# Differential attention and a convolution norm in a two-block transformer kernel: a group's end in three parts, the norm's small sums in two units

## What is computed

```python
def conv_mixer(u, w, b, gn_g, gn_b):          # 256 channels, 4 groups, 31 taps
    a, gt = jnp.split(u, 2, axis=-1)
    z = a * jax.nn.sigmoid(gt)
    y = causal_depthwise_conv(z, w) + b
    yf = y.reshape(B, S, CONV_GROUPS, CONV_CH // CONV_GROUPS)
    mu = jnp.mean(yf, axis=-1, keepdims=True)
    var = jnp.mean(jnp.square(yf - mu), axis=-1, keepdims=True)
    yn = ((yf - mu) * lax.rsqrt(var + EPS)).reshape(B, S, CONV_CH) * gn_g + gn_b
    return jax.nn.silu(yn)

def diff_attention(q, k, v, ...):             # 4 heads, two maps (m) each, D = 64
    s = jnp.einsum('bhmqd,bhmkd->bhmqk', qb, kh) * scale    # per block of 128 queries
    s = jnp.where(k_pos[None, :] <= q_pos[:, None], s, -jnp.inf)
    p = jax.nn.softmax(s, axis=-1)
    a = p[:, :, 0] - lam * p[:, :, 1]
    o = jnp.einsum('bhqk,bhkv->bhqv', a, vh)
    o = rms_norm_2(o, subln_g) * (1.0 - lambda_init)
```

## Time and profile before

| | us |
|---|---|
| median of three runs | 2995.51 |
| lowest and highest run | 2993.77, 3003.24 |
| span of the profiled execution | 3009.3 |
| PE busy in the span | 2916.2 |
| DVE, ACT, POOL busy | 1520.2, 1212.6, 1162.8 |

### The profile page before, as it was taken

The page is one execution under the profiler, slowest core; times in us unless marked ns, Lnnn a source line. Parts: engine busy times, 40 slices in busy tenths (PEclk is TensorE's granted clock), DMA queues, the critical chain, the costliest instruction groups (busy, mean ns, idle before and its releaser), DMA issues.

```text
span 3009.3 us, 37747 instructions
## 1 busy us (share of the span) xinstructions
PE 2916.2 (97%) x13529; PEld 2341.0 (78%) x13529; DVE 1520.2 (51%) x2650; ACT 1212.6 (40%) x1851; POOL 1162.8 (39%) x598
## 2 busy tenths in 40 slices
PE   9999999999999999999999999999999999997997
PEld 7888888767888888888888867778888777775664
DVE  4441365556744414344145655764441888457665
ACT  4332233665343322433232476443331353425563
POOL 4444353522454443544444351354454332012221
PEclk9999999999999999999999999999999999699998
DMA  4333232202323332333323311423332121016995
GB/s 151 97 98 107 82 130 82 63 25 89 114 91 98 103 106 64 98 98 98 104 83 123 91 41 36 126 81 105 98 104 96 52 88 57 22 63 247 344 359 196
DMA packets 118574, 324.15 MB, mean 108 GB/s; under 512 B 12464, under 2 KB 48688, under 8 KB 117936
## 3 DMA queue, kind: packets, MB, share of 16 engines
q1 hardware_dynamic: 109024, 305.17, 31.2%
q10 hardware_dynamic: 2800, 8.91, 0.8%
q0 software_dynamic: 6624, 8.41, 0.8%
HBM read 313.52 MB, written 24.64 MB: 112 GB/s over the span
## 4 chain that ended last, share of the span: by engine, by line
PE 85%; DVE 7%; ACT 3%; issue 2%; DMA 1%; POOL 1%; DVEq 0%; SPq 0%; ACTq 0%; POOLq 0%
PE ps L430 19%; PE ps L431 19%; PE ps L433 19%; PE ps L465 4%; PE ps L2165 3%; PE ps L1042 2%; PE ps L930 2%; PE ps L2151 1%; PE ps L2153 1%; PE ps L2152 1%; PE ps L1026 1%; PE ps L573 1%; PE ps L492 1%; PE ps L2137 1%; PE ps L919 1%
## 5 line engine op out<-in xcount | busy, mean ns | idle before, releaser
L2913 POOL TENSOR_TENSOR wlo<-raw,whi 128x1024 fp32r<-128x1024 f32 (+1 forms) x368 | 953.7, 2593 | 1415.5 <-ACT whi L628 1415.3
L628 ACT ACTIVATE whi<-raw 128x1024 fp32r<-128x1024 f32 (+1 forms) x368 | 409.2, 1112 | 693.1 <-PE ps L433 585.8
L430 PE MATMUL ps<-xlo,whi 128*128 128x512 f32 x1704 | 665.2, 390 | 2.2 <-POOL wlo L2913 1.6
L431 PE MATMUL ps<-xhi,wlo 128*128 128x512 f32 x1704 | 663.2, 389 | 0.0
L433 PE MATMUL ps<-xhi,whi 128*128 128x512 f32 x1704 | 420.8, 389 | 0.0
L430 PEld LDWEIGHTS ps<-xlo,whi 128*128 128x128 f32 x1704 | 320.0, 188 | 70.0 <-POOL wlo L2913 2.0
L433 PEld LDWEIGHTS ps<-xhi,whi 128*128 128x128 f32 x1704 | 319.8, 188 | 66.3
L431 PEld LDWEIGHTS ps<-xhi,wlo 128*128 128x128 f32 x1704 | 319.9, 188 | 65.9
L430 PE MATMUL ps<-hlo,whi 128*128 128x512 f32 x704 | 277.3, 394 | 0.0
L431 PE MATMUL ps<-hhi,wlo 128*128 128x512 f32 x704 | 275.5, 391 | 0.0
L760 DVE SCALAR_TENSOR_TENSOR xa<-ps,xa 128x512 f32<-128x512 f32 x48 | 33.1, 689 | 353.4 <-PE ps L433 350.6
(11 more groups left out here) (631 smaller groups left out, 4880.8 us busy)
## 6 DMA issues: line engine op xcount, KB each, us to landing
raw<-in_gu SPq DMA_DIRECT2D x176, 512.0 KB, 3.5
raw<-in_mix SPq DMA_DIRECT2D x96, 512.0 KB, 3.6
mraw<-in_w SPq DMA_DIRECT2D x23, 2048.0 KB, 12.4
raw<-in_dn SPq DMA_DIRECT2D x64, 704.0 KB, 4.1
mdraw<-in_w SPq DMA_DIRECT2D x23, 1024.0 KB, 13.5
raw<-in_w SPq DMA_DIRECT2D x32, 512.0 KB, 3.5
gate_rows<-tails SPq DMA_DIRECT2D x32, 256.0 KB, 4.3
sgmn<-gate_rows SPq DMA_DIRECT2D x16, 512.0 KB, 4.0
```

Source lines behind the costliest of these rows:

```text
L430: nc.tensor.matmul(out, whi[:, slot, cols], rlo, start=first and t == 0, stop=False)
L431: nc.tensor.matmul(out, wlo[:, slot, cols], rhi, start=False, stop=False)
L628: nc.scalar.activation(whi[:, s, 0:n], raw[:, r, 0:n], ACT.Copy).then_inc(hi_done, 1)
L2913: nc.gpsimd.tensor_tensor(wlo[:, s, 0:n], raw[:, r, 0:n], whi[:, s, 0:n].bitcast(F32), ALU.subtract).then_inc(w_ready, 1)
```

## The change

A group's end is done in three parts: the first (reciprocals and the first weighted half) behind the maximum at which all of it stood before, the second (the other half and the addition) behind the next maximum, the third (the two sums of squares) behind the one after. The convolution norm's mean moves from u = 4 to u = 5 (`CONV_MEAN`), its sixteen small sums at u = 8 become eight at u = 9 and eight at u = 10, in different banks, and the roots, two in place of one, are taken by ACT at u = 10, which PE's units 11 and 12 wait for. DVE's reciprocal and both copies stand at u = 11 (before: u = 9 and 10). ACT's casts in the units move from u = 1, 4, 8, 12, 16 to u = 4, 6, 9, 13, 16.

```diff
 def dve_units(..., steps=1):
-        for u in range(n + lag):
+        for u in range(n + lag + steps - 1):
...
-            t = u - lag
-            if t >= 0 and t % per == per - 1:
-                dve.wait_ge(S["o_ready"], t + 1)
-                grp = t // per
-                finish(grp, stat[:, 32 + 16 * (grp % 2):32 + 16 * (grp % 2) + per])
+            for step in range(steps):
+                t = u - lag - step
+                if 0 <= t < n and t % per == per - 1:
+                    grp = t // per
+                    sums = stat[:, 32 + 16 * (grp % 2):32 + 16 * (grp % 2) + per]
+                    if step == 0:
+                        dve.wait_ge(S["o_ready"], t + 1)
+                    if steps == 1:
+                        finish(grp, sums)
+                    else:
+                        finish(grp, sums, step)
...
+    OUT_CAST = (6, 9, 13, 16)
...
-        if u == CONV_MEAN + 3:
+        if u == CONV_MEAN + 2:
             pe.wait_ge(S["norm_dve"], 1)
...
-    CONV_MEAN, CONV_AT = 4, 12
+    CONV_MEAN, CONV_AT = 5, 12
...
-        if u == CONV_MEAN + 4:
-            pe.wait_ge(S["sq_ready"], 2)
-            for k in range(2):
-                for kt in range(QT):
-                    at_ = 256 + 8 * k + 2 * kt
-                    ins = nc.tensor.matmul(ps[2][:, at_:at_ + 2], rs2[:, k, kt * P:(kt + 1) * P],
-                                           c("blk64")[:, 0:128:64], start=True, stop=True)
+        k = u - CONV_MEAN - 4
+        if k in (0, 1):
+            pe.wait_ge(S["sq_ready"], k + 1)
+            for kt in range(QT):
+                at_ = 256 + 2 * kt
+                ins = nc.tensor.matmul(ps[2 + u % 2][:, at_:at_ + 2], rs2[:, k, kt * P:(kt + 1) * P],
+                                       c("blk64")[:, 0:128:64], start=True, stop=True)
             ins.then_inc(S["stat_used"], 1)
-        if u == CONV_MEAN + 6:
-            pe.wait_ge(S["std_ready"], 1)
+        if k in (2, 3):
+            pe.wait_ge(S["std_ready"], k - 1)
...
-        if u == 1:
+        if u == 4:
             hi(act, B2, N_IN2_TILES + 3, 0, 8)
...
-        if u == CONV_MEAN + 4:
-            act.wait_ge(S["stat_used"], 1)
-            nc.scalar.activation(conv_r, ps[2][:, 256:272], ACT.Sqrt, bias=eps_ap(RMS_EPS)).then_inc(S["std_ready"], 1)
+        if u == CONV_MEAN + 5:
+            for k in range(2):
+                act.wait_ge(S["stat_used"], k + 1)
+                nc.scalar.activation(conv_r[:, 8 * k:8 * k + 8], ps[2 + (u + 1 + k) % 2][:, 256:264], ACT.Sqrt,
+                                     bias=eps_ap(RMS_EPS)).then_inc(S["std_ready"], 1)
...
-        if u % 4 == 0 and 4 <= u <= 16:
-            hi(act, B2, G2_OUT + u // 4 - 1, 0, 8)
+        if u in OUT_CAST:
+            hi(act, B2, G2_OUT + OUT_CAST.index(u), 0, 8)
...
-        if u == CONV_MEAN + 5:
-            dve.wait_ge(S["std_ready"], 1)
+        if u == CONV_MEAN + 6:
+            dve.wait_ge(S["std_ready"], 2)
             own.link(nc.vector.reciprocal(conv_r, conv_r))
             own.wait()
...
+        def finish_dif(grp, sums, step):
...
+            if step == 0:
+                own.link(nc.vector.reciprocal(w, sums))
+                own.wait()
+                own.link(nc.vector.tensor_tensor(w2[:, :, 1], w2[:, :, 1], small[:, 4:5].broadcast_to([P, 2]), ALU.mult))
+                own.wait()
+                own.link(weighted(0))
+            elif step == 1:
+                weighted(1).then_inc(S["o_used"], 1)
+                dve.wait_ge(S["o_used"], grp + 1)
+                own.wait()
+                own.link(nc.vector.tensor_tensor(o, o, other, ALU.add))
+            else:
+                own.wait()
+                for h in range(2):
+                    r = 4 * (grp // 2) + 2 * (grp % 2) + h
+                    own.link(nc.vector.tensor_tensor_reduce(sg[:, 0, 256 + P * h:256 + P * h + P], o[:, h, :], o[:, h, :],
+                                                           1.0, 0.0, ALU.mult, ALU.add, rt3[:, r:r + 1]))
```

More of the change, by code:

```diff
@@ L953, in act_units, with dve_units @@
                 between(u)
-    def dve_units(dve, units, scale, per, finish, own, s_ring=s_ring, between=None):
+    def dve_units(dve, units, scale, per, finish, own, s_ring=s_ring, between=None, steps=1):
         n = len(units)
         lag = 4
-        for u in range(n + lag):
+        for u in range(n + lag + steps - 1):
             if u < n:
@@ L2036, in dve_late @@
             cols = slice(256 * half, 256 * half + 256)
-            nc.vector.tensor_tensor(cacc[:, 1, cols], cacc[:, 1, cols], ps[2 + half][:, 256:512], ALU.subtract
+            nc.vector.tensor_tensor(cacc[:, 1, cols], cacc[:, 1, cols], ps[2 + u % 2][:, 256:512], ALU.subtract
                                     ).then_inc(S["norm_dve"], 1)
-        if u == CONV_MEAN + 5:
-            dve.wait_ge(S["std_ready"], 1)
+        if u == CONV_MEAN + 6:
+            dve.wait_ge(S["std_ready"], 2)
             own.link(nc.vector.reciprocal(conv_r, conv_r))
             own.wait()
-        if u in (CONV_MEAN + 5, CONV_MEAN + 6):
-            k = u - CONV_MEAN - 5
-            nc.vector.tensor_copy(rs2[:, k, :].rearrange("p (a c) -> p a c", c=64),
-                                  conv_r[:, 8 * k:8 * k + 8].unsqueeze(2).broadcast_to([P, 8, 64])
-                                  ).then_inc(S["conv_wide"], 1)
+            for k in range(2):
+                nc.vector.tensor_copy(rs2[:, k, :].rearrange("p (a c) -> p a c", c=64),
+                                      conv_r[:, 8 * k:8 * k + 8].unsqueeze(2).broadcast_to([P, 8, 64])
+                                      ).then_inc(S["conv_wide"], 1)
         if CONV_AT <= u < CONV_AT + 4:
@@ L2521, in between @@
             dve_late(dve, own, u)
-        def finish_dif(grp, sums):
+        def finish_dif(grp, sums, step):
             w = stat[:, 104:108]
-            own.link(nc.vector.reciprocal(w, sums))
-            own.wait()
             w2 = w.rearrange("p (h m) -> p h m", m=2)
-            own.link(nc.vector.tensor_tensor(w2[:, :, 1], w2[:, :, 1], small[:, 4:5].broadcast_to([P, 2]), ALU.mult))
-            own.wait()
             o = o_dif[:, grp // 2, 256 * (grp % 2):256 * (grp % 2) + 256].rearrange("p (h d) -> p h d", d=P)
@@ L2531, in finish_dif @@
             other = sg[:, 0, 0:256].rearrange("p (h d) -> p h d", d=P)
-            for m in range(2):
-                ins = nc.vector.tensor_tensor((o, other)[m], dif_bank(grp, 0)[:, 256 * m:256 * m + 256].rearrange("p (h d) -> p h d", d=P),
-                                              w2[:, :, m:m + 1].broadcast_to([P, 2, P]), ALU.mult)
-                if m == 0:
-                    own.link(ins)
-                else:
-                    ins.then_inc(S["o_used"], 1)
-            dve.wait_ge(S["o_used"], grp + 1)
@@ L2540, in finish_dif, with weighted @@
-            own.wait()
-            own.link(nc.vector.tensor_tensor(o, o, other, ALU.add))
-            own.wait()
-            for h in range(2):
-                r = 4 * (grp // 2) + 2 * (grp % 2) + h
-                own.link(nc.vector.tensor_tensor_reduce(sg[:, 0, 256 + P * h:256 + P * h + P], o[:, h, :], o[:, h, :], 1.0,
-                                                       0.0, ALU.mult, ALU.add, rt3[:, r:r + 1]))
-        dve_units(dve, dif_units, dif_scale, 4, finish_dif, own, s2_ring, between=between)
+            def weighted(m):
+                return nc.vector.tensor_tensor((o, other)[m],
+                                               dif_bank(grp, 0)[:, 256 * m:256 * m + 256].rearrange("p (h d) -> p h d", d=P),
+                                               w2[:, :, m:m + 1].broadcast_to([P, 2, P]), ALU.mult)
@@ L2548, in dve_second @@
+        dve_units(dve, dif_units, dif_scale, 4, finish_dif, own, s2_ring, between=between, steps=3)
         own.wait()
```

2 lines of the change are left out of this document (1 added, 1 removed).

## The result

The kernel with the change takes 2984.35 us (median of 8 runs, 2979.55 to 2989.09). The kernel before, run beside it, takes 2999.89 (8 runs, 2993.72 to 3013.20; the three runs known ahead are among them). The ratio is 0.9946, with a 95% interval of 0.9927 to 0.9965: some 16 us faster. The four later batches of this study hold 98 runs of the kernel before, with a median of 3000.8 (2988.8 to 3011.1); the change has a median of 2985.0 over all its 16 runs, 15.9 less. The forecast was 2981.8 us, and it named "faster" as likeliest.

A forecast was written before the change was run, and what follows sets the result against it. TensorE was taken as the bound, busy 2916.2 of 3009.3 us. Terms -7.7 - 1.7 + 1.3 - 1.1 - 4.5 = -13.7 us, carried over to the median 2995.5, gave 2981.8 us; 8 in 10 range 2965 to 2996.

The forecast's parts named there:

- Taps and mean: -7.7: Convolution taps of u = 1 and the mean's products: taps 2.1 us shorter, TensorE's clock stays up; -7.7 us.
- "-3" for the case without the clock: At the taps, if the clock falls all the same: only 2.1 us of taps and about 1 of reordering, -3.
- Sums and roots: -1.7 + 1.3 = -0.4: Small sums from u = 8: no clock fall behind them, -1.7 us; new TensorE wait for the root at u = 11, +1.3.
- Group's end: -1.1: Units 15 to 17: split end cuts TensorE's wait for unit 14's copy from 1.50 to about 0.4 us; -1.1 us.
- the early-fall rival: Attention tail: POOL's low part delays the sums of squares at u = 17, clock falls; 2986.3 us; 0.27 with fall at taps.
- the port: DVE instructions with two SBUF inputs and SBUF-reading GpSimd share a port; a rule against the change at the casts' units.
- To the states: -4.5: From 2585.2 us to the state products: no clock fall, -5.7, less a longer wait for values' rows, +1.2; -4.5 us.
- Behind that: 0: Behind the state products: clock falls at ACT's tables and sigmoids, then all goes as before to 2639.8; 0 us.
- the rival of a clock that stays up: Clock stays up to the attention stage's end: another -14 us, 2967.7 us; chance 0.13.
- The carrying over: Whole kernel: the sum from the profiled span, -13.7 us, applied unchanged to the runs' median 2995.5, giving 2981.8 us.
- The slower case: Root wait at u = 11 brings the clock down, work between 2572 and 2585 doubles, +12.7 + 1.3; 3007.4 us; chance 0.06.

The follow-up runs named there:

- second look at before: The kernel before, unchanged, run again for a second profile; 2993.52 us.
- the end whole: The changed kernel with the group's end in one piece again behind one maximum, casts and norm as in the change; 2993.42 us, ratio 0.9981.
- full-clock execution: The changed kernel, unchanged, run again for a second profile, its whole attention stage at full clock; 2985.41 us, ratio 0.9940.

## Why the prediction held, step by step

**Taps and mean: -7.7, and 8.0 in the profile.** The mark at u = 8 moves by 9.8 us (32.7 to 22.9), of which 1.84 are the small sums that now stand behind it. The tap time (2.73) and the first wait (1.15 forecast, 1.17 measured) came as said, and the mean's products waited for nothing. The second look at before shows what it is made of: 3.7 us are clock and the other 4.3 the shorter taps and the order. Where I put "-3" for the case without the clock, it is -4.3. In medians, undoing the casts costs 7.9 and undoing the norm 4.2.

**Sums and roots: -1.7 + 1.3 = -0.4, and -0.3 in the profile.** From u = 8 to 12 it takes 13.6 us in place of 12.1, with 1.9 us of small sums more in it. The root wait was 1.46 for 1.3. But the reason for the -1.7 fails: in the second look at before the clock did not fall there and the four units took 12.0 us, as long as with the fall. ACT's copy at u = 10 set the pace, and a wait of 1.16 took the place of the low time. The low stretch had cost nothing. What paid for the root's wait was something I had not counted: the cast of u = 8 had stood in ACT between the root and the exponential's table, and with the casts moved alone the four units take 11.0 us and the wait of 1.16 is gone. That the sum came out is chance.

**Group's end: -1.1, and -1.34.** 0.16 us of wait for my 0.4. The sums of squares took 0.28 us each, ended 0.2 us before POOL's low part at u = 17 and held nobody up, so the early-fall rival did not come. They did not run side by side, so this place shows nothing of the port. The Trainium skill (SBUF — State Buffer, "Who interferes with whom") says that whichever of the two starts first has the port; the profile with the end whole agrees: there POOL's low part starts 0.64 us ahead of the addition, keeps its usual 2.39 us, and the addition, 2.03 us in place of 0.42, ends 0.3 us behind it. In runs the split is worth more than this term: 8.4 us of the median. What is more than the wait goes with the falls that it keeps away, which the sum carries in the next term.

**To the states: -4.5.** I expected no fall at 2585.2 (right) and a wait of 1.7 for the values' rows (1.45 measured). To the maximum of u = 20 the terms make -8.1 - 1.1 - 4.4 (half of the 8.85 us from 2585.2 to 2594.05) = -13.6; the mark moved by 13.2.

**Behind that: 0, and -11.6 in the profile.** Here the step fails. The clock fell where I said, behind ACT's tables, but "from then to 2639.8 all goes as before" did not hold: it rose after 6.8 us in one execution and did not fall in the other. The profile is therefore nearer to the rival of a clock that stays up. That the median moved by 15.9 and not by some 25 has its reason in the other profile of before: the long low stretch to 2639.8 belonged to that execution. Before's second look stands 8.8 us behind the change at u = 20 and 10.6 behind its full-clock execution at u = 28. The 0 was wrong for the profile and nearly right for the runs. That is luck: I had taken one execution's low stretch for the program's.

**The carrying over.** I set -13.7 against 2995.51, a median of three. Over 98 runs it is 3000.8. Against that the same sum gives 2987.1; the change measures 2985.0. The sum was 2 us too small and the base 5 too low; the two work against each other, and the forecast came out 3 us below.

**The slower case** (the root wait brings the clock down for long) did not come in either profile of the change. Eight profiles here have the root wait of about 1.46. In one of them, with the end whole, about 4 us at a mean clock of 0.57 lie behind it, and they cost 1.6 us: the scores of u = 11 start 32.88 us behind the first against 32.69 in the change, those of u = 12 37.64 against 35.85. So the wait can bring the clock down, for far less than the 12.7 us of the rival. Taking that wait away wasn't tried, since the sums and the scores share a bank; it stays open what it is worth.

## What to carry to other kernels

Where an engine's clock is granted by what it does, cost a wait by what the clock does behind it, and find all the waits that bring it down: of the three parts here two gave about half of the gain each and one nothing that could be measured, when each was done alone. Low-clock time is a cost only where that engine sets the pace; check for each low stretch whether the next wait would just grow. Before a sum is built on one profile, look at how far the runs lie apart: of a kernel whose runs spread by 20 us a single execution shows where the stalls are, not what they cost on average, and a dozen runs leave 5 us open on the value of a part.
